# Hybrid decoder layer on one core: gate matmuls, probability copies, expert rows and first merge strips of the large token group placed anew

## The reference

```python
def reference(x, ...):
    for l in range(DEPTH):                       # DEPTH = 1
        mix = hybrid_mixer(x, ...)
        x = layer_norm(ALPHA * x + mix, ...)
        ffn = peer_ffn(x, ...)
        x = layer_norm(ALPHA * x + ffn, ...)

def hybrid_mixer(x, ...):
    h = einsum('bsd,de->bse', x, w_in)           # one projection to all parts
    y_fox = forgetting_attention(...)            # 8 heads of 64, causal, with decay
    y_swa = sliding_window_gqa(...)              # window 128, 8 heads, 2 key groups
    y_pool, y_conv = multiscale_pool(...), conformer_conv(...)
    gates = sigmoid(gl.reshape(B, S, 4, D))
    merged = (gates[:, :, 0] * (y_fox @ p_fox) + gates[:, :, 1] * (y_pool @ p_pool)
              + gates[:, :, 2] * (y_conv @ p_conv) + gates[:, :, 3] * (y_swa @ p_swa))
    return merged @ w_out

def peer_ffn(x, w_q, sub_k1, sub_k2, u_tab, v_tab):
    # per token and head: 16 of 128 x 128 experts by two key scores -> idx, softmax g
    act = gelu(einsum('cd,ced->ce', xb, u_tab[ib]))
    return einsum('ce,ced->cd', gb * act, v_tab[ib])     # 128 experts per token
```

## Time and profile before

| | |
|---|---|
| median of 3 runs | 3710.17 us (3702.59 to 3712.28) |
| the profiled execution | 3718.67 us, of which the trace spans 3716.9 us |
| PE busy | 3175.3 us (85%) |
| DVE busy | 2672.2 us (72%) |
| POOL, ACT busy | 1574.0 us (42%), 836.4 us (23%) |
| transfers | 1073.17 MB, mean 289 GB/s |

### The profile page before, as it was taken

The page is one execution under the profiler, slowest core; times in us unless marked ns, Lnnn a source line. Parts: engine busy times, 40 slices in busy tenths (PEclk is TensorE's granted clock), DMA queues, the critical chain, the costliest instruction groups (busy, mean ns, idle before and its releaser), DMA issues.

```text
span 3716.9 us, 40306 instructions
## 1 busy us (share of the span) xinstructions
PE 3175.3 (85%) x14137; PEld 1748.0 (47%) x14161; DVE 2672.2 (72%) x5156; ACT 836.4 (23%) x2013; POOL 1574.0 (42%) x1321
## 2 busy tenths in 40 slices
PE   7579889987888795884899899898999999889970
PEld 5458545755555563542444344444444444333430
DVE  5755449976777665867778896978947874545779
ACT  6334212122121121210110272653810000000000
POOL 5100001124655434434534343435425667777564
PEclk9779999997889797997999999999999999999995
DMA  8469434356878747985869889989899999999996
GB/s 279 139 235 368 184 130 136 109 162 226 280 269 281 264 169 249 380 319 205 318 265 365 298 303 364 326 323 342 307 387 362 384 379 347 325 342 358 407 410 256
DMA packets 313258, 1073.17 MB, mean 289 GB/s; under 512 B 36704, under 2 KB 62944, under 8 KB 309216
## 3 DMA queue, kind: packets, MB, share of 16 engines
q0 software_dynamic: 170704, 606.75, 45.1%
q1 hardware_dynamic: 101904, 363.16, 26.4%
q10 hardware_dynamic: 40448, 100.68, 7.5%
HBM read 931.52 MB, written 138.94 MB: 288 GB/s over the span
## 4 chain that ended last, share of the span: by engine, by line
PE 17%; DMA 14%; POOL 12%; DVE 5%; issue 4%; ACT 1%; DVEq 0%; ACTq 0%; POOLq 0%
PE ps L1781 13%; DMA rows<-v,expert_ids 6%; POOL rows L133 5%; POOL hidden_sums L1746 4%; POOL turned_rows L133 3%; DMA rows<-u,expert_ids 3%; DMA turned_rows<-u,expert_ids 1%; DMA h_side_kept<-mixer_state 1%; DMA turned_rows<-v,expert_ids 1%; DVE rows L162 1%; PE ps L107 1%; PE ps L109 1%; PE ps L108 1%; DVE row_sums L168 1%; DMA mixer_state<-u_t 1%
## 5 line engine op out<-in xcount | busy, mean ns | idle before, releaser
L133 POOL DMA_INDIRECT rows<-u,expert_ids x477 | 581.7, 1219 | 851.3 <-DVE hidden_sums L162 726.9
L1781 PE MATMUL ps<-turned_rows,mixer_state 128*128 128x512 f32 x2048 | 899.7, 598 | 7.3 <-DMA mixer_state<-u_t 6.6
L133 POOL DMA_INDIRECT rows<-v,expert_ids x527 | 609.6, 1157 | 673.3 <-DVE row_sums L168 513.7
L168 DVE SCALAR_TENSOR_TENSOR row_sums<-rows,hidden_sums,row_sums 128x1024 f32<-128x1024 f32 x518 | 654.4, 1282 | 253.7 <-DMA rows<-v,expert_ids 248.5
L1818 PE MATMUL ps<-shared_64k 128*128 128x512 f32 x1536 | 674.8, 602 | 41.1 <-DVE shared_64k L1945 41.0
L1781 PEld LDWEIGHTS ps<-turned_rows,mixer_state 128*128 128x128 f32 x2048 | 388.1, 192 | 479.4 <-issue 469.3
L1818 PEld LDWEIGHTS ps<-shared_64k 128*128 128x128 f32 x1536 | 295.2, 193 | 420.6 <-issue 420.6
L162 DVE CUSTOM_DVE_ANT_0 rows<-rows,x_first 128x1024 f32<-128x1024 f32 x256 | 305.8, 1221 | 47.1 <-DMA rows<-u,expert_ids 44.8
L107 PE MATMUL ps<-x_hi_t_b,shared_64k 128*128 128x384 f16 x912 | 312.4, 343 | 18.4 <-DMA shared_64k<-w_pairs_kept 17.6
L162 DVE CUSTOM_DVE_ANT_0 rows<-rows,branches 128x1024 f32<-128x1024 f32 x221 | 268.7, 1219 | 73.8 <-DMA rows<-u,expert_ids 71.4
L108 PE MATMUL ps<-x_lo_t_b,shared_64k 128*128 128x384 f16 x912 | 310.9, 341 | 0.0
(11 more groups left out here) (526 smaller groups left out, 4990.3 us busy)
## 6 DMA issues: line engine op xcount, KB each, us to landing
mixer_state<-u_t ACTq DMA_DIRECT2D x128, 512.0 KB, 6.9
shared_64k<-v SPq DMA_DIRECT2D x128, 512.0 KB, 7.2
rows<-strips SPq DMA_DIRECT2D x32, 768.0 KB, 7.1
h_kept<-branches ACTq DMA_DIRECT2D x32, 768.0 KB, 10.5
shared_64k<-weights_kept SPq DMA_DIRECT2D x32, 768.0 KB, 8.9
shared_64k<-h_kept SPq DMA_DIRECT2D x32, 768.0 KB, 12.9
shared_64k<-s_pairs_kept SPq DMA_DIRECT2D x32, 512.0 KB, 6.6
rows<-w_t SPq DMA_DIRECT2D x30, 512.0 KB, 5.6
```

Of the source, the lines that this page charges most:

```text
L133: nc.gpsimd.indirect_dma_start(row_tile(M, n), None, A["u" if r < NSEL else "v"], bass.IndirectOffsetOnAxis(ap=M["idx"][:, c, e:e + 1], ax ...
L168: nc.vector.scalar_tensor_tensor(acc[:, e % 2, :], src, hid[:, c % 2, e:e + 1], acc[:, e % 2, :], ALU.mult, ALU.add).then_inc(used, 1)
L1781: m = pe.matmul(ps[:, 4 + u % 4, 0:UT], uk[u % 4][:, k, :], x1t[:, k, :], start=k == 0, stop=k == KD - 1)
```

## The change

1. `FILL_STEPS`: gate matmuls at all steps except `bare_unit` (the second head of the two longest query blocks, 8 of 48 units). The 52 half strips then end at step 59 instead of 63: 40 instead of 36 in units, 2 at steps 48 and 49 as before, and 10 instead of 14 in the window attention, whose last two rounds have none.
2. The copy of the first transposed group moves from DVE to ACT (in both groups: 48 units of group B and 16 of group A).
3. Rows: by length of unit (3, 4, 4, 4, 5, 5 per unit, 2 for a bare one, each taken one step after its unit), 6 instead of 9 per round of window attention; merge tail 6, 6, 6, 5, 3, 0 instead of 5, 5, 5, 5, 5, 3. Over the stages: attention 257 rows to 221, merge 92 to 90, scores 56 to 52, `ffn` 712 to 754. The gelu of the second token block moves from the end of the merge to the fourth score row.
4. `ROWS_U_BLOCK` 2.9 to 3.1 and `ROWS_V_BLOCK` 2.1 to 2.2. From the end of the scores to the first product DVE now takes 394 rows instead of 369, from there to the last product 275 instead of 262, and after it 85 instead of 81.
5. The first two merge strips have SBUF of their own and are loaded at the end of the attention block.
6. Group A's projection has 6 buffers for split weights instead of 3.
7. The three dense layer norms stand 12, 8 and 4 rows ahead of the last row instead of after it.

```diff
+def bare_unit(u):
+    return u < N_UNIT_B and u // 2 % GB.nc >= GB.nc - 2 and u % 2 == 1
+def unit_rows(u):
+    if u >= N_UNIT_B:
+        return 3
+    return 2 if bare_unit(u) else (3, 4, 4, 4, 5, 5)[u // 2 % GB.nc]
-FILL_STEPS = [s for s in range(N_UNIT_B + 2 + 2 * (GB.nc + 1)) if s >= N_UNIT_B or s % 4 != 3]
+FILL_STEPS = [s for s in range(N_UNIT_B + 2 + 2 * (GB.nc + 1)) if not bare_unit(s)][:FILL]
-ATT_ROWS = spans_of(PROJ_ROWS[-1][1], [0] + [4] * (N_UNIT_B + 2) + [9] * (GB.nc + 1))
-MERGE_ROWS = spans_of(ATT_ROWS[-1][1], [2] * ITEMS + [5] * GB.nc)
+ATT_ROWS = spans_of(PROJ_ROWS[-1][1], [0] + [unit_rows(u) for u in range(N_UNIT_B + 2)] + [6] * (GB.nc + 1))
+MERGE_ROWS = spans_of(ATT_ROWS[-1][1], [2] * ITEMS + [6, 6, 6, 5, 3, 0])
...
# attention, SP, after the gate strips
+            for i in range(2):
+                sp.dma_start(M["pair"][i], A["s_pairs"][i][:, :, KD:KD + 4, :]).then_inc(M["first_strips"], 16)
...
# attention, ACT: all groups
-                if a:
-                    if u >= 2:
-                        act.wait_ge(pv, u - 1)
-                    copied(act.activation(pt[u % 2][:, a:a + nblk, :].rearrange("p a b -> p (a b)"),
-                                          bank[:, 0:P * nblk], ACT.Copy), k)
+                if a == 0 and u >= 2:
+                    act.wait_ge(pv, u - 1)
+                copied(act.activation(pt[u % 2][:, a:a + nblk, :].rearrange("p a b -> p (a b)"),
+                                      bank[:, 0:P * nblk], ACT.Copy), k)
...
# merge, SP and PE: items 0 and 1 are not loaded again
+                if i < 2:
+                    pe.wait_ge(M["first_strips"], 32)
+                else:
+                    pe.wait_ge(s_in[i % NPAIR], 16 * (i // NPAIR + (i % NPAIR == 2)))
...
-ROWS_U_BLOCK = 2.9
-ROWS_V_BLOCK = 2.1
+ROWS_U_BLOCK = 3.1
+ROWS_V_BLOCK = 2.2
...
+DENSE_NORM_AT = {NROW - 12 + 4 * _d: _d for _d in range(ND)}
...
         for n in range(R_SCORE, NROW):
+            if n in DENSE_NORM_AT:
+                dense_norm(DENSE_NORM_AT[n])
...
-            M["wp"] = [s1(f"w_pair_{i}", [P, 2, KD, P], F16)[:] for i in range(3)]
+            M["wp"] = [s1(f"w_pair_{i}", [P, 2, KD, P], F16)[:] for i in range(6)]
```

More of the change, by code:

```diff
@@ L236, in project @@
     w_in = [sem(f"w_in{i}") for i in range(3)]
-    w_st = [sem(f"w_stored{i}") for i in range(3)]
+    w_st = [sem(f"w_stored{i}") for i in range(6)]
     x_in = [sem(f"x_in{i}") for i in range(2)]
@@ L1033, in copy_group @@
             bank = ps[:, 4 + k % 2, :]
-            if kind == "p":
-                _, u, a, nblk = groups[k]
-                if a == 0:
-                    dve.wait_ge(t_done, k + 1)
-                    if u >= 2:
-                        dve.wait_ge(pv, u - 1)
-                    copied(nc.vector.tensor_copy(pt[u % 2][:, 0:nblk, :].rearrange("p a b -> p (a b)"),
-                                                 bank[:, 0:P * nblk]), k)
-            elif kind == "y":
+            if kind == "y":
                 _, j, q = groups[k]
@@ L1093, in _ @@
                     zeros[:, 0:W], -SC, 3e38, ALU.add, ALU.min, nb[:, u % 4:u % 4 + 1]).then_inc(s_read, 1)
-            if 1 <= u <= NU:
-                for k in fox_groups[u - 1]:
-                    copy_group(k)
             if 2 <= u <= NU + 1:
@@ L1193, in item_load @@
             def item_load(i):
-                sp.dma_start(pair[i % NPAIR], A["s_pairs"][i][:, :, KD:KD + 4, :]).then_inc(s_in[i % NPAIR], 16)
+                if i >= 2:
+                    sp.dma_start(pair[i % NPAIR], A["s_pairs"][i][:, :, KD:KD + 4, :]).then_inc(s_in[i % NPAIR], 16)
                 sp.dma_start(sg[i % NSG], A["gates"][i]).then_inc(gate_in[i % NSG], 16)
@@ L1832, in high @@
             act.activation(hp[i % 2][0], ps[:, 0:2, :].rearrange("p a b -> p (a b)"), ACT.Copy).then_inc(t_hi, 1)
+        gelus = gelu_points(SCORE_ROWS)
         for i in range(4):
@@ L1844, in _ @@
                 act.activation(stage[:, 512 * q:512 * q + 512], ps[:, 6 + q % 2, :], ACT.Copy, scale=RWS).then_inc(s_out, 1)
+            if i in gelus:
+                gate_hidden(act, M, gelus[i])
         gate_exps(act, M, S, 0)
@@ L1959, in _, with dense_norm @@
             use_rows(nc, dve, M, *SCORE_ROWS[i])
+        def dense_norm(d):
+            if d == 0:
+                dve.wait_ge(v_mm, NBLK)
+                dve.wait_ge(again_in, 16 * ND)
+            nc.vector.scalar_tensor_tensor(again[d], again[d], ALPHA,
+                                           ps[:, 2 + 2 * d:4 + 2 * d, :].rearrange("p a b -> p (a b)"), ALU.mult, ALU.add)
+            dve.drain()
+            layer_norm(nc, dve, M, again[d]).then_inc(dense_done, 1)
         for n in range(R_SCORE, NROW):
+            if n in DENSE_NORM_AT:
+                dense_norm(DENSE_NORM_AT[n])
             for c, a, b in CHOICE_AT.get(n, ()):
@@ L1971, in _ @@
                 second_norm(row_at(n)[0])
-        for d in range(ND):
-            if d == 0:
-                dve.wait_ge(v_mm, NBLK)
-                dve.wait_ge(again_in, 16 * ND)
-            nc.vector.scalar_tensor_tensor(again[d], again[d], ALPHA,
-                                           ps[:, 2 + 2 * d:4 + 2 * d, :].rearrange("p a b -> p (a b)"), ALU.mult, ALU.add)
-            dve.drain()
-            layer_norm(nc, dve, M, again[d]).then_inc(dense_done, 1)
 def pair_view(ap):
@@ L2052, in mixer @@
         late()
+    own = ExitStack()
+    if not g.first:
+        first = own.enter_context(nc.sbuf_tensor("first_strips_b", [P, 2, 2, 4, P], F16))
+        M["pair"] = [first[:, i] for i in range(2)] + [pair_tile(big, 1024, 4)]
     with ExitStack() as c2:
@@ L2085, in mixer @@
         else:
-            M["pair"] = [pair_tile(big, 512 * i, 4) for i in range(3)]
             M["wo"] = [big[:, 8192 + 1024 * k:9216 + 1024 * k].bitcast(F16).rearrange("p (a c) -> p a c", a=2)
@@ L2098, in mixer @@
         merge(nc, c3, M, A, g)
+    own.close()
 def pair_tile(big, at, k):
@@ L2165, in build_mix @@
     M["stage_sems"] = {}
-    M["values_in"] = sem("values_in")
+    M["values_in"], M["first_strips"] = sem("values_in"), sem("first_strips")
     M["mp_in"] = [sem(f"folded_in{i}") for i in range(4)]
```

2 lines of the change are left out of this document (removed).

## The result

The changed kernel takes 3724.55 us (median of five runs, 3710.51 to 3733.17) where the kernel before takes 3702.59 (3696.37 to 3712.28) beside it: ratio 1.005, 95% interval 1.0027 to 1.0073. A second set of runs gave 1.0062 (1.0039 to 1.0085). The change makes the kernel half a per cent slower, where 3659 was forecast and no more than 3700 allowed for.

The account below looks back on a forecast made before the run. No engine was full in the attention units, where PE and DVE waited for each other; u and v phases held PE almost full. Gains of 98 us less losses of 47 gave 51, so 3659 us; range 3605 to 3700, own range 3625 to 3690.

Parts of the forecast that it names:

- attention units: Attention units, 418 us before: forecast 362 us, a gain of 56, with ends of 88 and 1.
- window attention and first merge product: Window attention: 26 us gained, mostly in its last two rounds; first merge product 9 us sooner through early strips.
- merge items; mix: Merge: about 1 us gained by half a megabyte less to transfer, and 2.6 us by two rows less in its tail.
- u phase to the first product: u phase: 394 rows instead of 369 before the first product, 25 us lost; ends 5 and 57.
- the ends: Best and worst values given for the stages' terms, such as 88 and 1 us for the units' gain.
- ACT takes the copies: Attention units: DVE's copies, 32 us by DVE's price, go to ACT, which is busy 80 of 418 us.
- I keep a third of that, 33 us: Attention units: of 54 us idle and some 50 us of slow clock, a third was taken to remain.
- floor of 329 us: Attention units: least time for both PE, with four more gate matmuls, and DVE, about 329 us.
- this case (3714): Rival: eight units without gate matmul become holes where PE waits, 55 us above forecast, 3714 us; chance 0.06.
- The fourth rival: Attention units: PE waits for ACT behind the exponential instead, 41 us above forecast, 3700 us; chance 0.04.
- The two waits of PE that were to tell: u and v phases, lines 1799 and 1818 before: well over 130 us in all instead of 79 would show the forecast wrong.
- the rival of rows at POOL's pace: u and v phases: each moved row costs 2.9 us, 122 us for 42, giving 3734 us; chance 0.07.

Follow-up runs that it names:

- old_copies_behind: Kernel before the change with all probability copies on ACT, behind the exponential as in the change; 3710.0 us, ratio 1.001, units 427.6 us.
- dve_copies: Changed kernel with the copy of each unit's first group back on DVE, right after the row maxima; 3709.5 us, ratio 1.003, units 421.7 us.
- copies_ahead: Changed kernel with ACT's copies of the previous unit put ahead of the next unit's exponential; 3662.4 us, ratio 0.991, again 3665.8; units 356.5 and 361.7 us.
- rows_shifted: Changed kernel with the expert-row list moved one step, so bare steps have 2 rows beside them, not 5; 3688.9 us, ratio 0.997, units 389.1 us.
- ahead_old_rows: copies_ahead with the row lists and block rates of the kernel before the change; 3656.0 us, ratio 0.987, units 379.9 us.
- mix_front: ahead_old_rows with the mix's 28 rows as 6, 6, 6, 6, 4, 0 instead of 5, 5, 5, 5, 5, 3; 3646.4 us, ratio 0.986.
- window_rows: ahead_old_rows with 44 instead of 60 rows in the window attention, 14 more behind the scores; 3653.6 us, ratio 0.988.
- more_rows_early: Changed kernel with copies ahead and rows shifted, plus 5 instead of 4 rows for the fourth unit length, `ROWS_U_BLOCK` 3.02; 3683.4 us, ratio 0.994.

## Why the prediction was wrong

Each term, with the means of two traces of each kernel:

| term | forecast | measured |
|---|---|---|
| up to the units (group A's projection) | -4 | -8 (845.7 and 857.3, then 843.7 and 843.8) |
| attention units | -56 | -2 |
| window attention and first merge product | -26 - 9 | -30 |
| merge items; mix | -1; -2.6 | -5; -12 |
| scores | 0 | +1 |
| u phase to the first product | +25 | +28 |
| first to last product | +14 | +21 |
| last product to the end | +8 | +8 |
| sum | -51 | +2 |

The traces thus put the two kernels 2 us apart and the medians 22: both traces of the kernel before lie 9 to 16 us above its median, and the first of the changed kernel 14 below its own. In which stage the other runs differ no run here shows. The 8 us up to the units are not settled, as the two traces of the kernel before differ by 12 there.

The forecast also started from 3710.2, the median of three runs; five sets have the kernel before at 3697 to 3705. And its own range, 3625 to 3690, does not come out of the ends: half of the way to each of them, added up, gives 3617 to 3718, and the measured time lies beyond that too.

**The units: the step that failed.** "ACT takes the copies" counted ACT's time (80 of 418 us busy) and not its order, and "I keep a third of that, 33 us" supposed the mutual waits would mostly go with DVE's copy. They stayed, since the copy was late on DVE for the reason for which it is late on ACT: on DVE it stands behind the next row maxima, on ACT behind the exponential that waits for them. old_copies_behind and dve_copies show that the engine makes no difference to the units, copies_ahead that the place does. With the copies ahead the units take 357 and 362 us. The forecast had 362 by borders that count 9 us less (418 and 427 before the change), so its floor of 329 us and 33 us of loss were near what a kernel takes in which most of the wait is gone. Of the 73 us between the forecast (51 less) and the medians (22 more), moving the copies ahead gives back 59. The count of rows was wrong as well: by equal borders 15 rows left the units, not 12.

**The bare units.** The prediction priced this case (3714) and set it aside with the argument that "the 5-row step stands beside the bare PE step and the next has 2 rows, so the maxima come early". It is the other way round: rows in a step delay the maxima after them. The five rows beside the bare step make the next maxima late just where PE has no gate matmul to wait behind; rows_shifted shows 32 us for this. The fourth rival, copies that only change hands, describes the same waits (41.8 us for ACT now, 43.0 for DVE before) and had a chance of 0.04. Each of the two rivals had half of what happened: waits for ACT's copy, most of them at the bare steps. What was needed to see it stood in the order rows ahead of the prediction: the copies right below the exponential.

**Window attention and merge.** 30 us against 35: nearly the right sum from the wrong parts. The gate matmuls that left the last rounds and the early strips give a few us at most (ahead_old_rows and mix_front have both, and 216.0 and 208.6 us; kernels with neither have 212.8 to 216.9). The rows give most of it: 19 to 26 us for 16 in window_rows, and the change takes 21 out of this stretch (67 to 46 between the last scaling and the first product), where the prediction had put most on the gates. With the early strips the product comes 15.0 to 17.1 us after DVE's last instruction, in the changed kernel 17.1, instead of 19.7: some 3 to 5 us, not 9, because the border between two blocks was forgotten. Timelines of the changed kernel there, DVE and SP:

```profile
1434.97 1.23 DVE L187 SCALAR_TENSOR_TENSOR x_first<-x_first,row_sums 128x1024 f32<-128x1024 f32 x1
1453.28 1.02 DVE L1345 SCALAR_TENSOR_TENSOR shared_64k<-ps,shared_64k 128x384 f32<-128x384 f32 x2 [17.08 <-PE ps L122]
```

```profile
1446.18 0.80 SPq L1199 DMA_DIRECT2D shared_64k<-gates_kept  x2
```

DVE is done at 1436.2, and SP issues the first gate load at 1446.2: ten microseconds lie ahead of the 8.8 of landing on which the 11 us of the forecast rested.

**Mix.** Two rows at 1.3 us were counted; 12 us came. What matters is what DVE has left when PE's last mix matmul is done, and 6, 6, 6, 5, 3, 0 puts the rows beside PE's work. mix_front shows it at equal count.

**u and v phases, tail.** Right in mechanism, and somewhat too small, 47 us where the runs show 56 to 63. The tail is right (the last product was at 3571.25 of 3716.9 and now stands at 3554.33 of 3708.7: 145.6 us became 154.4). With the old rows and the new places of the norms it is 150.4 and 151.0 us, so about half of the growth is the four rows. The two waits of PE that were to tell, in the two phases of the changed kernel, against the earlier trace rows:

```profile
PE ps L1826 <- DVE shared_64k L1956: 57.9, 13, 16.5
PE ps L1807 <- ACT branches L1879: 47.6, 9, 11.9
```

105.5 us instead of 79, in the second trace 120.7: more, and short of the 130 that were to mark the rival of rows at POOL's pace. The longest, 16.5 us, is that for the first product. The Trainium skill, "Trainium Kernel Development and Optimization", Key Constraints, from which the prediction drew an estimate of 1.4 us a row and 60 us for 42, comes nearer than the prediction's own sum: 56 to 63 us are 1.3 to 1.5 us a row. The 14 rows of window_rows at 0.7 to 1 us each don't settle that transfers are the reason.

## What to carry to other kernels

On an engine that works in order, ask of each instruction what waits ahead of it: a copy that others need goes ahead of the instruction that itself waits for a third engine. Changing the engine alone did not help here; DVE's own copy ahead of its row maxima was not run, so which engine is better then stays open. Filler work is paid for by its place as well as its count: beside a short step of the engine that others wait for it delays what comes next, beside a long one it costs less, though not nothing (more_rows_early). A planned list's offset to the step that it runs beside is worth checking in a timeline before arguing from it.

## What was not expected

- One row of DVE's 1.3 us costs 1.2 to 2.7 us in the units (18 to 27 us for 15 rows, 21.6 for 8), 1.2 to 1.6 in the window attention (19 to 26 for 16), and 0.7 to 1.5 late, though DVE is idle for a quarter of the units. These are differences between single traces.
- A wait of 5 us of PE costs twice: itself, and the lower clock level after it (2.4 us more for the next gate matmul). Units with 42 us of such waits ran at a granted clock of 0.88, with 9 us at 0.97.
- The profiled execution of copies_ahead was the fastest of its ten, 3638.6 us, at 0.929 the highest granted clock over the span. The second trace, 3653.3 us, has the same units within 6 us, so that their gain was not that run's luck.
